# A large fused transformer kernel on one core: 40 blocks of weights under HGRN's levels multiplied in float32 straight from the ring, in place of two float32r parts

## The chip, the cores and the metric

The kernel runs on 1 core of a Trainium2 chip. The metric is the device time of one execution in microseconds (us). Before the change the median of 3 runs is 2754.78 us (2750.23 to 2757.37). Engines are named as in the profile: PE is TensorE (matrix products), PEld its weight load, DVE VectorE, ACT ScalarE, POOL GpSimd, and SP the engine that issues the weight loads from HBM.

## The reference, cut to what matters

Two transformer blocks on 256 tokens of width 1024, all in float32. The change touches the mixer of the second block alone. It projects the normalized input `xn` (256 x 1024) with `w_in` into q, zf_fwd, zf_bwd, v (`inp`), an output gate og, three Hyena channels and two branch gates:

```python
proj = jnp.einsum('bld,dc->blc', xn, w_in)
q, zf_fwd, zf_bwd, inp, og, hy, gates = jnp.split(proj, IN_SPLITS, axis=-1)
```

q goes through Silu, og through Silu and the gates through a sigmoid. zf_fwd and zf_bwd give the decays and keys of HGRN2, a linear attention with a decay per channel (8 heads of 128), run forward and backward over the tokens; its output, per head, is a decayed product of q, keys and v.

## The kernel before, in words

The program is a list of steps in one order, written by a planner in Python. Every engine follows this list and does its own part of each step, in order; semaphores (`Mark`) join the engines. So what an engine does next is fixed by the order of planning, and an instruction that waits holds up all that is planned behind it on its engine.

**Weights.** They come in blocks of 128 x 1024 float32 (512 KB), 8 k-slices of 128 x 128. A block is a `Split` step (L294): SP loads it into one of 3 ring slots (`weight_ring`, L313), ACT rounds it to float32r, the high part (L317), and the remainder, the low part, is a subtraction on DVE (L322) or on POOL (L328), as `c.low_by` says. The two parts go into one of 3 buffers (`weight_parts`). The slot is free again when the low part is made; the buffer, when PE has multiplied the block. `product` (L346 to L351) makes each product as three matmuls: high x high, high x low, low x high. `xn` itself lies as such parts (`acts_high`, `acts_low`), made by `Normalize`; its unrounded value lies in `work`, which nothing reads until HGRN's heads write their output there.

**Jobs.** `submit` (L242) plans the load and split of a block and puts its multiplication in a list; it plans the multiplication of the block that is then more than 2 behind (`AHEAD = 2`). `flush` (L253) plans the first blocks of the next group and all multiplications that are left. `Channels` (L354) multiplies a block into 128 channels x 256 tokens, `TokenUnit` (L393) a block into 2 x 128 tokens x 512 columns (four units make one half of v). `Keep` (L444, its activation at L457) evacuates the bank on ACT. In this stage the blocks have three banks in rotation (`c.rotation = [4, 5, 6]`); banks 0 to 3 belong to HGRN.

**The stage.** In `second_mixer` (L2520) the blocks of zf and zb come first, with the low parts on DVE. Then `c.low_by` is set to "pool", and `together` plans one step of `hgrn` and one step of the filler `more` by turns. `more` submits 40 blocks: 8 of q, 8 of v, then 8 of og and 16 of the two gates (`gate_a`, `gate_b`). `hgrn` (L2165) plans:

- `HgrnKeys`: sigmoids on ACT (L1997, L1998), scalings on DVE (L2007, L2008, L2012), a logarithm on ACT (L2001), once for zf and once for zb;
- `HgrnScan`: 16 scans over the tokens on DVE (L2025, L2026), and a memset on POOL (L2036);
- 9 levels (block sizes 128, 64, 32, 16, 8, 4, 2, 1 and 0), in pairs by `pipeline` with width 2. A level subtracts the decays on DVE (L2067 to L2074), exponentiates them on ACT (L2109, L2111), multiplies them into q and the keys on DVE (L2078, L2081, L2082), makes 16 score products on PE in float32 in two halves of 8 (L2131) and keeps them on DVE (L2097, L2098, L2100); level 0 only adds the keys (L2087);
- 8 `HgrnHead` steps: 4 float32 matmuls each (L2151 to L2154), and a copy to `work` on ACT (L2158).

The filler is out of step with the levels by two blocks (`AHEAD`): behind the scores of the first pair come units 1 to 3 of v and their evacuation, then the exponentials of the second pair; behind those of the third pair come three blocks of og and their evacuations, then the exponentials of the fourth. When the levels are done, 7 blocks are left; before the change they alternate with the heads. Then come the first two splits for Hyena (`w[32]`, `w[40]`), and a barrier (L596).

Of the kernel before, what the change touches and what calls it, by code (L numbers as in the profile page):

```python
# [9 lines left out]
NT, KD = T // P, D // P  # L10
# [89 lines left out]
class Signal:  # L100


    def __init__(self, name, handle, by=1):
        self.name, self.handle, self.by, self.counted, self.sent = name, handle, by, 0, 0
# [19 lines left out]
class Step:  # L124
# [4 lines left out]
    def sync(self, q):  # L129
        pass  # L130
# [30 lines left out]
def pipeline(c, makers, width):  # L161

    makers, active = list(makers), {}
    for slot in range(min(width, len(makers))):
        step = makers.pop(0)(slot)
        active[slot] = [step, step.phases]
    while active:
        for slot in list(active):
            if not active[slot][1]:
                if not makers:  # L170
                    del active[slot]
                    continue
                step = makers.pop(0)(slot)
                active[slot] = [step, step.phases]
            c.plan(active[slot][0])
            active[slot][1] -= 1
        yield


def together(main, filler, every):  # L180

    for n, _ in enumerate(main):
        if n % every == 0:
            next(filler, None)


class Parts:

    def __init__(self, high, low):
        self.high, self.low, self.marks, self.free = high, low, [None] * KD, None


class Core:
# [4 lines left out]
    def __init__(self, nc, ctx, dram):  # L200
        self.nc, self.ctx, self.dram = nc, ctx, dram
        self.steps, self.signals = [], {}
        self.psum = ctx.enter_context(nc.psum_tensor("psum", [P, 4096], F32))
        self.ring = self.sb("weight_ring", [P, self.SLOTS, 1024])
        self.parts = self.sb("weight_parts", [P, self.PARTS, 2, 1024], dtype=F32R)
        self.landed = [self.sig(f"slot_landed_{i}", 16) for i in range(self.SLOTS)]
        self.slot_free = [None] * self.SLOTS
        self.part_free = [None] * self.PARTS
        self.bank_free = [()] * 8
        self.rotation = list(range(7))  # L210
        self.loaded = self.splits = self.n_small = 0
        self.low_by = "vector"
        self.jobs, self.prepared = [], []
        self.small_before = [None] * 16
        self.fence = ()
# [23 lines left out]
    def load(self, out, src, after=()):  # L239
        return self.plan(Load(self, out, src, after)).came  # L240

    def submit(self, src, make):  # L242

        unit = self.prepared.pop(0) if self.prepared else self.plan(Split(self, src)).unit
        self.jobs.append((unit, make))
        if len(self.jobs) > self.AHEAD:
            self.work_off()
# [4 lines left out]

    def flush(self, *following):  # L253
        for src in following:
            self.prepared.append(self.plan(Split(self, src)).unit)
            if self.jobs:
                self.work_off()
        while self.jobs:
            self.work_off()
# [31 lines left out]
    pass  # L291


class Split(Step):  # L294


    def __init__(self, c, src):
        self.src, self.unit = src, Unit()
        u, slot, part = self.unit, c.loaded % c.SLOTS, c.splits % c.PARTS
        c.loaded += 1  # L300
        c.splits += 1
        u.part = part
        self.ring, self.slot_free, self.part_free = c.ring[:, slot, :], c.slot_free[slot], c.part_free[part]
        self.high, self.low = c.parts[:, part, 0, :], c.parts[:, part, 1, :]
        self.low_by = c.low_by
        self.landed = c.landed[slot].next()
        self.rounded = c.mark("weights_high")
        u.ready = c.mark("weights_low_by_" + self.low_by)
        c.slot_free[slot] = u.ready
# [36 lines left out]
def product(q, out, stationary, moving, first, last):  # L346

    (sh, sl), (mh, ml) = stationary, moving
    q.e.matmul(out, sh, mh, start=first, stop=False)  # L349
    q.e.matmul(out, sh, ml, start=False, stop=False)  # L350
    return q.e.matmul(out, sl, mh, start=False, stop=last)  # L351


class Channels(Step):  # L354


    def __init__(self, c, unit, acts, evac):
        self.unit, self.acts, self.evac = unit, acts, evac
        self.weights = c.parts[:, unit.part, :, :].rearrange("p x (k c) -> p x k c", k=KD)
        b = c.take_bank()  # L360
        self.out, self.bank_free = c.bank(b)[:, 0:T], c.bank_free[b]
        self.marks = list(acts.marks)
        self.done = c.part_free[unit.part] = acts.free = c.mark("multiplied")
        c.last_product = self.done
        c.bank_free[b] = (evac.out_of_psum(c),)

    def tensor(self, q):
        w, acts = self.weights, self.acts
        q.wait_ge(self.unit.ready, *self.bank_free)
        for k in range(KD):  # L370
            q.wait_ge(self.marks[k])
            last = product(q, self.out, (w[:, 0, k, :], w[:, 1, k, :]), (acts.high[:, k, :], acts.low[:, k, :]),
                           k == 0, k == KD - 1)
        last.then_inc(*self.done.once())

    def scalar(self, q):
# [16 lines left out]
class TokenUnit(Step):  # L393

    def __init__(self, c, whole, unit, n):
        self.whole, self.unit, self.n = whole, unit, n
        self.weights = c.parts[:, unit.part, :, :].rearrange("p x (k c) -> p x k c", k=whole.n_k)
        if n == 0:
            whole.banks = [c.take_bank() for _ in range(NT)]
            whole.bank_free = [m for b in whole.banks for m in c.bank_free[b]]  # L400
            whole.out = [c.bank(b)[:, 0:whole.cols] for b in whole.banks]
        self.marks = list(whole.acts.marks)
        self.done = c.part_free[unit.part] = whole.acts.free = c.mark("multiplied")
        c.last_product = self.done
        self.final = n == whole.n_units - 1
        if self.final:
            self.evacs = [whole.evac(i) for i in range(NT)]
            for b, evac in zip(whole.banks, self.evacs):
                c.bank_free[b] = (evac.out_of_psum(c),)

    def tensor(self, q):
        whole, w, acts = self.whole, self.weights, self.whole.acts
        q.wait_ge(self.unit.ready)
        if self.n == 0:
            q.wait_ge(*whole.bank_free)
        for i in range(NT):
            tile = slice(P * i, P * i + P)
            for kk in range(whole.n_k):
                k = whole.n_k * self.n + kk
                q.wait_ge(self.marks[k])  # L420
                last = product(q, whole.out[i], (acts.high[:, k, tile], acts.low[:, k, tile]),
                               (w[:, 0, kk, :], w[:, 1, kk, :]), k == 0, k == KD - 1)
        last.then_inc(*self.done.once())

    def scalar(self, q):
# [1711 lines left out]
class HgrnHead(Step):  # L2137


    def __init__(self, c, s, hd, v, o):  # L2140
        self.c, self.s, self.hd, self.v, self.after, self.o = c, s, hd, v, list(s.kept) + list(s.values), o
        self.b = hd % 4
        self.bank_free = c.bank_free[self.b]
        self.mixed, self.taken = c.mark("hg_mixed"), c.mark("hg_taken")
        c.bank_free[self.b] = (self.taken,)
# [8 lines left out]
        q.e.matmul(out[:, P:T], v1, s.at[:, hd, 1, :], start=False, stop=True).then_inc(*self.mixed.once())  # L2154

    def scalar(self, q):
        q.wait_ge(self.mixed)
        q.e.activation(self.o[:, self.hd, :], self.c.bank(self.b)[:, 0:T], ACT.Copy).then_inc(*self.taken.once())  # L2158


# [1 line left out]
    pass  # L2162


def hgrn(c, ctx, s, q, zf, zb, projected, v, o):  # L2165

    lb = c.sb("hg_lb", [P, KD], ctx)
    one_minus = c.sb("hg_one_minus", [P, KD], ctx)
# [22 lines left out]
    s.operands_free, s.kept = [(), ()], [None, None]  # L2191

    yield from pipeline(c, [lambda u, n=n, m=m: HgrnLevel(c, s, n, m, u) for n, m in enumerate([P] + LEVELS + [0])], 2)
    for hd in range(HG_H):
        c.hg_taken = c.plan(HgrnHead(c, s, hd, v, o)).taken
        yield


# [321 lines left out]
def second_mixer(c, h, xn, work, tmp, following):  # L2520

    w = c.dram["w_in_2"]
    with ExitStack() as ctx:
# [6 lines left out]
        with ExitStack() as inner:  # L2530
# [8 lines left out]
                c.channels(w[8 + n], xn, Keep(zf[:, n, :]))  # L2539
            for n in range(KD):  # L2540
                c.channels(w[16 + n], xn, Keep(zb[:, n, :]))
            c.flush(w[0], w[1])
            projected = c.last_kept
            c.rotation = [4, 5, 6]
            c.low_by = "pool"
            s = Hgrn()

            def more():
# [15 lines left out]
                        yield  # L2564

            filler = more()
            together(hgrn(c, inner, s, q, zf, zb, projected, v, o), filler, 1)
            for _ in filler:
                pass
            c.flush(w[32], w[40])  # L2570
            c.barrier()
        gated_ready = c.plan(Activate(c, og[:, :, :], ACT.Silu, c.last_kept)).ready
        for x in (sga, sgb):
# [123 lines left out]
def program(nc, dram, out):  # L2697
    with ExitStack() as ctx:
        c = Core(nc, ctx, dram)
        h = c.sb("h", [P, KD, T])  # L2700
        xn = Parts(*(c.sb(f"acts_{x}", [P, KD, T], dtype=F32R) for x in ("high", "low")))
        work = c.sb("work", [P, KD, T])
        tmp = c.sb("tmp", [P, T])
        c.gains = c.sb("gains", [P, N_GAINS])
        c.ident = c.sb("ident", [P, P])
# [138 lines left out]
```

## Time and profile before

| | |
|---|---|
| median of 3 runs | 2754.78 us |
| the profiled execution | 2750.74 us |
| its span, first to last instruction | 2749.0 us |
| mean granted clock of PE | 0.935 |
| DVE, ACT, POOL busy, share of the span | 65%, 43%, 33% |
| low parts on POOL (L328) | x314, 808.2 us, mean 2582 ns |
| roundings on ACT (L317) | x702, 736.3 us, mean 1049 ns |
| the chain that ended last | PE 75%, DVE 16%, POOL 3%, ACT 3% |

The granted clock is a share of 2.4 GHz; 0.5 is 1.2 GHz. PE's matmuls are pipelined and their records overlap, so the time of one is read from the distance between starts. A float32 matmul leaves two records of weight load and two of multiplication, a float32r matmul one of each.

A row of the timeline has the start in us, the duration in us, the engine, the line, the operation, output <- inputs, the form and how many were merged; in brackets, the idle time before it and what ended it. A row of the chain has start, duration, engine, output and line. A row of the table by stretch of time has the stretch, its length, then busy us (and instructions) of PE, PEld, DVE, ACT and POOL, the granted clock, the share of the DMA engines and GB/s.

### The profile page before, as it was taken

Reading aid. Unit: us, or ns where it says so; the run is one execution under the profiler, and the core shown is the slowest. Engines: PE = TensorE matmul, PEld = TensorE weight load, DVE = VectorE, ACT = ScalarE, POOL = GpSimd, SP = SyncE. Lnnn points to the kernel's source line nnn. Section 1 sums busy time; section 2 is a strip of 40 time slices with the busy share of each in tenths; the row PEclk is TensorE's granted clock in tenths of the full one; section 3 lists DMA queues with packets and bytes.
Section 4 is the critical chain, followed back from the end, with each engine's and each line's share of the span. In section 5 each row is a group of like instructions: output and inputs, shape, how many; then the busy total and the mean of one; then the engine's idle time right before and its main releaser. Section 6 shows DMA issues by size and latency. Waiting matters only on the chain.

```text
span 2749.0 us, 39097 instructions
## 1 busy us (share of the span) xinstructions
PE 2468.2 (90%) x16062; PEld 2233.6 (81%) x16062; DVE 1800.3 (65%) x2703; ACT 1191.1 (43%) x1925; POOL 895.9 (33%) x418
## 2 busy tenths in 40 slices
PE   6866978999999999998867878888999999999997
PEld 5855868999999888886856877578999999888885
DVE  4544444997888655555587547364996888655555
ACT  3422333445444444443544354324445444444443
POOL 2011010797666200001054545110797666200000
PEclk8856988999999999999978898989999999999999
DMA  5210433455444556664422343234455444566663
GB/s 162 92 62 23 125 98 119 150 175 160 146 147 146 165 187 189 188 187 153 123 77 84 101 123 109 85 108 161 146 172 161 147 145 147 168 190 186 189 187 112
DMA packets 108569, 384.41 MB, mean 140 GB/s; under 512 B 13007, under 2 KB 16000, under 8 KB 107816
## 3 DMA queue, kind: packets, MB, share of 16 engines
q1 hardware_dynamic: 108392, 381.91, 45.4%
q8 instruction: 129, 2.11, 0.3%
q14 instruction: 48, 0.39, 0.0%
HBM read 380.79 MB, written 1.06 MB: 139 GB/s over the span
## 4 chain that ended last, share of the span: by engine, by line
PE 75%; DVE 16%; POOL 3%; ACT 3%; issue 2%; DMA 1%; SPq 0%; DVEq 0%; POOLq 0%; ACTq 0%
PE psum L349 21%; PE psum L350 20%; PE psum L351 20%; PE psum L1741 4%; POOL weight_parts L328 2%; PE psum L511 1%; PE psum L2358 1%; PE psum L2131 1%; DVE peer_experts L1649 1%; PE psum L795 1%; PE psum L1220 1%; ACT weight_parts L317 1%; DVE peer_experts L1648 1%; DVE peer_experts L1625 1%; DVE peer_experts L1617 1%
## 5 line engine op out<-in xcount | busy, mean ns | idle before, releaser
L349 PE MATMUL psum<-acts_high,weight_parts 128*128 128x256 f32 x3296 | 972.9, 295 | 65.9 <-DVE acts_low L543 28.4
L328 POOL TENSOR_TENSOR weight_parts<-weight_ring,weight_parts 128x1024 fp32r<-128x1024 f32 x314 | 808.2, 2582 | 551.5 <-ACT weight_parts L317 550.9
L350 PE MATMUL psum<-acts_low,weight_parts 128*128 128x256 f32 x3296 | 945.0, 287 | 0.0
L351 PE MATMUL psum<-acts_high,weight_parts 128*128 128x256 f32 x3296 | 944.0, 286 | 0.0
L317 ACT ACTIVATE weight_parts<-weight_ring 128x1024 fp32r<-128x1024 f32 x702 | 736.3, 1049 | 112.8 <-PE psum L351 109.5
L349 PEld LDWEIGHTS psum<-acts_high,weight_parts 128*128 128x128 f32 x3296 | 643.7, 195 | 83.4 <-issue 42.4
L322 DVE TENSOR_TENSOR weight_parts<-weight_ring,weight_parts 128x1024 fp32r<-128x1024 f32 x388 | 477.0, 1230 | 308.4 <-ACT weight_parts L317 308.4
L350 PEld LDWEIGHTS psum<-acts_low,weight_parts 128*128 128x128 f32 x3296 | 645.5, 196 | 2.4 <-issue 1.7
L351 PEld LDWEIGHTS psum<-acts_high,weight_parts 128*128 128x128 f32 x3296 | 644.4, 196 | 0.0
L349 PE MATMUL psum<-weight_parts,peer_coef 128*128 128x512 f32 x1024 | 405.9, 396 | 4.0 <-issue 3.9
L350 PE MATMUL psum<-weight_parts,peer_coef 128*128 128x512 f32 x1024 | 405.6, 396 | 0.0
L351 PE MATMUL psum<-weight_parts,peer_coef 128*128 128x512 f32 x1024 | 405.6, 396 | 0.0
L1812 ACT ACTIVATE peer_coef<-peer_experts 128x256 fp32r<-128x256 f32 x256 | 106.6, 417 | 363.9 <-PE psum L351 362.8
L489 POOL TENSOR_TENSOR peer_experts<-h 128x256 f32<-128x256 f32 x16 | 9.7, 612 | 746.6 <-DVE h L473 746.4
L1725 DVE TENSOR_TENSOR peer_onehots<-peer_onehots,peer_gates 128x512 f32<-128x512 f32 x128 | 247.9, 1936 | 4.4
L349 PEld LDWEIGHTS psum<-weight_parts,peer_coef 128*128 128x128 f32 x1024 | 192.7, 188 | 51.0 <-issue 4.2
L350 PEld LDWEIGHTS psum<-weight_parts,peer_coef 128*128 128x128 f32 x1024 | 192.9, 188 | 46.8
L351 PEld LDWEIGHTS psum<-weight_parts,peer_coef 128*128 128x128 f32 x1024 | 192.8, 188 | 46.6
L1816 DVE TENSOR_TENSOR peer_coef<-peer_experts,peer_coef 128x256 fp32r<-128x256 f32 x256 | 109.6, 429 | 161.2 <-ACT peer_coef L1812 161.2
L1722 DVE TENSOR_TENSOR peer_onehots<-psum,peer_pairs 128x1024 f32<-128x1024 f32 x128 | 155.2, 1212 | 0.1
L1789 ACT ACTIVATE psum<-psum 128x4 f32<-128x4 f32 (+25 forms) x156 | 41.4, 266 | 248.7 <-PE psum L351 248.7
L1791 ACT ACTIVATE peer_experts<-psum 128x256 f32<-128x256 f32 (+32 forms) x250 | 79.3, 317 | 151.2 <-PE psum L351 151.1
(382 smaller groups left out, 2426.3 us busy)
## 6 DMA issues: line engine op xcount, KB each, us to landing
weight_ring<-in_peer_down SPq DMA_DIRECT2D x128, 512.0 KB, 3.6
weight_ring<-in_peer_up SPq DMA_DIRECT2D x128, 512.0 KB, 3.6
weight_ring<-in_peer_u SPq DMA_DIRECT2D x128, 512.0 KB, 3.6
weight_ring<-in_peer_v SPq DMA_DIRECT2D x128, 512.0 KB, 4.1
weight_ring<-in_w_in SPq DMA_DIRECT2D x88, 512.0 KB, 3.6
weight_ring<-in_w_out SPq DMA_DIRECT2D x16, 512.0 KB, 3.5
weight_ring<-in_peer_w_q SPq DMA_DIRECT2D x16, 512.0 KB, 3.6
weight_ring<-in_w_in_v SPq DMA_DIRECT2D x10, 512.0 KB, 3.5
```

The source lines that it names most:

```text
L317: q.e.activation(self.high, self.ring, ACT.Copy).then_inc(*self.rounded.once())
L322: q.e.tensor_tensor(self.low, self.ring, self.high.bitcast(F32), ALU.subtract).then_inc(*self.unit.ready.once())
L328: q.e.tensor_tensor(self.low, self.ring, self.high.bitcast(F32), ALU.subtract).then_inc(*self.unit.ready.once())
L349: q.e.matmul(out, sh, mh, start=first, stop=False)
L350: q.e.matmul(out, sh, ml, start=False, stop=False)
L351: return q.e.matmul(out, sl, mh, start=False, stop=last)
L1722: q.e.tensor_tensor(self.hot, over(over(self.c.bank(7)[:, 0:P], GROUP, 1), 2, 1), over(x.pairs[:, :, tokens], P, 3), ALU.is_equal).then_in ...
L1725: q.e.tensor_tensor(self.hot[:, 0, :, :], self.hot[:, 0, :, :], over(x.gates[:, tokens], P, 2), ALU.mult).then_inc(*self.ready.once())
L1741: last = q.e.matmul(out, self.hot[:, 0, t, :], self.hot[:, 1, t, :], start=True, stop=True)
L1791: last = q.e.activation(self.x.experts[:, self.n, n:T], out[:, n:T], ACT.Gelu_apprx_tanh)
L1812: q.e.activation(self.high, self.src, ACT.Copy).then_inc(*self.rounded.once())
L1816: q.e.tensor_tensor(self.low, self.src, self.high.bitcast(F32), ALU.subtract).then_inc(*self.ready.once())
```

## The change

The 40 blocks of the filler are planned as `Whole` steps: SP loads them into the ring, and nothing else is done to them. PE multiplies them in float32 from the ring slot with the unrounded activations in `work` (`xn.whole`); one matmul stands where three stood. The slot is free again only when PE has multiplied the block. `c.whole` is set before the first two blocks of q are prepared, and taken back in `finish`, which `hgrn` now calls between the levels and the heads: it plans what is left of the filler (7 blocks) and the two splits for Hyena, whose low parts are made by POOL. So all heads come behind the last block. Since a head writes to `work`, its copy on ACT waits for the last whole block (`o_free`).

```diff
@@ class Core @@
+    def fetch(self, src):
+        return self.plan(Whole(self, src) if self.whole else Split(self, src)).unit
+
     def submit(self, src, make):
-        unit = self.prepared.pop(0) if self.prepared else self.plan(Split(self, src)).unit
+        unit = self.prepared.pop(0) if self.prepared else self.fetch(src)
...
+class Whole(Step):
+    def __init__(self, c, src):
+        self.src, self.unit = src, Unit()
+        slot = c.loaded % c.SLOTS
+        c.loaded += 1
+        self.ring, self.slot_free = c.ring[:, slot, :], c.slot_free[slot]
+        self.unit.whole, self.unit.slot, self.unit.ready = self.ring, slot, c.landed[slot].next()
+
+    def sync(self, q):
+        q.wait_ge(self.slot_free)
+        q.e.dma_start(self.ring, self.src).then_inc(*self.unit.ready.once())
...
@@ class Channels @@
-        self.done = c.part_free[unit.part] = acts.free = c.mark("multiplied")
+        self.done = c.mark("multiplied")
+        if unit.whole is None:
+            self.weights = c.parts[:, unit.part, :, :].rearrange("p x (k c) -> p x k c", k=KD)
+            c.part_free[unit.part] = acts.free = self.done
+        else:
+            self.weights = unit.whole.rearrange("p (k c) -> p k c", k=KD)
+            c.slot_free[unit.slot] = acts.whole_free = self.done
...
-            last = product(q, self.out, (w[:, 0, k, :], w[:, 1, k, :]), (acts.high[:, k, :], acts.low[:, k, :]),
-                           k == 0, k == KD - 1)
+            if self.unit.whole is None:
+                last = product(q, self.out, (w[:, 0, k, :], w[:, 1, k, :]), (acts.high[:, k, :], acts.low[:, k, :]),
+                               k == 0, k == KD - 1)
+            else:
+                last = q.e.matmul(self.out, w[:, k, :], acts.whole[:, k, :], start=k == 0, stop=k == KD - 1)
...
@@ class TokenUnit @@
+                    last = q.e.matmul(whole.out[i], acts.whole[:, k, tile], w[:, kk, :], start=k == 0,
+                                      stop=k == KD - 1)
...
@@ class HgrnHead @@
     def scalar(self, q):
-        q.wait_ge(self.mixed)
+        q.wait_ge(self.mixed, self.o_free)
...
@@ def hgrn @@
     yield from pipeline(c, [lambda u, n=n, m=m: HgrnLevel(c, s, n, m, u) for n, m in enumerate([P] + LEVELS + [0])], 2)
+    o_free = finish()
     for hd in range(HG_H):
-        c.hg_taken = c.plan(HgrnHead(c, s, hd, v, o)).taken
+        c.hg_taken = c.plan(HgrnHead(c, s, hd, v, o, o_free)).taken
         yield
...
@@ def second_mixer @@
+            c.whole = True
             c.flush(w[0], w[1])
             projected = c.last_kept
             c.rotation = [4, 5, 6]
-            c.low_by = "pool"
...
-            together(hgrn(c, inner, s, q, zf, zb, projected, v, o), filler, 1)
-            for _ in filler:
-                pass
-            c.flush(w[32], w[40])
+
+            def finish():
+                for _ in filler:
+                    pass
+                c.whole = False
+                c.low_by = "pool"
+                c.flush(w[32], w[40])
+                return xn.whole_free
+
+            together(hgrn(c, inner, s, q, zf, zb, projected, v, o, finish), filler, 1)
             c.barrier()
```

## Rows read from the trace of the kernel before

**Rows 1.** The page's first part: busy time of each engine over the span.
```profile
PE 2468.2 (90%) x16062; PEld 2233.6 (81%) x16062; DVE 1800.3 (65%) x2703; ACT 1191.1 (43%) x1925; POOL 895.9 (33%) x418
```

**Rows 2.** Busy time by stretch of time: the columns, the stage, one block at 1381.
```profile
core 0: us, PE busy (x) PEld busy (x) DVE busy (x) ACT busy (x) POOL busy (x), PEclk, DMA share, GB/s
1363.00:1598.00 235.00, 169.19 (x1192) 162.46 (x1191) 157.39 (x131) 103.08 (x112) 116.41 (x40) 0.83 0.29 88
...
1381.00:1386.00 5.00, 4.96 (x24) 4.70 (x23) 2.99 (x6) 2.93 (x3) 0.00 (x0) 0.52 0.32 105
```

**Rows 3.** Timeline of DVE and of POOL among the scans.
```profile
1399.89 1.80 POOL L2036 MEMSET hg_scores<- 128x2048 f32 x1
1401.66 5.48 POOL L328 TENSOR_TENSOR weight_parts<-weight_ring,weight_parts 128x1024 fp32r<-128x1024 f32 x2
...
1401.01 0.66 DVE L2026 TENSOR_TENSOR_SCAN hg_bb<-reset,hg_zb 128x256 f32<-128x256 f32 x1
1402.17 2.83 DVE L2026 TENSOR_TENSOR_SCAN hg_bb<-reset,hg_zb 128x256 f32<-128x256 f32 x1
```

**Rows 4.** Timeline of DVE and of POOL in the second pair of levels.
```profile
1451.39 2.28 DVE L2078 TENSOR_TENSOR hg_zf<-hg_q,hg_zf 128x2048 f32<-128x2048 f32 x1
...
1458.03 4.44 DVE L2078 TENSOR_TENSOR hg_q<-hg_q 128x2048 f32<-128x2048 f32 x1
...
1454.44 10.23 POOL L328 TENSOR_TENSOR weight_parts<-weight_ring,weight_parts 128x1024 fp32r<-128x1024 f32 x3 [7.46 <-ACT weight_parts L317]
```

**Rows 5.** Waits in the stage: who waited for whom, total, times, longest.
```profile
PE psum L349 <- POOL weight_parts L328: 15.3, 2, 12.8
```

**Rows 6.** The chain of waits: one float32r product; 16 float32 matmuls of 512 columns.
```profile
1549.11 0.12 PE psum L349
...
1762.03 13.75 PE psum L2358 x32
```

**Rows 7.** Timeline of PE: first and last of 27 rows of Hyena, float32, 256 columns.
```profile
1799.45 0.59 PE L2432 MATMUL psum<-sin_js,filters 128*128 128x256 f32 x2
...
1810.67 0.59 PE L2432 MATMUL psum<-sin_js,filters 128*128 128x256 f32 x2
```

**Rows 8.** The page's last part, DMA issues: w_in's blocks, KB each, us to landing.
```profile
weight_ring<-in_w_in SPq DMA_DIRECT2D x88, 512.0 KB, 3.6
```

**Rows 9.** Timeline of ACT: the two logarithms, and the fourth pair's first exponential.
```profile
1375.09 1.91 ACT L2001 ACTIVATE hg_zf<-hg_zf 128x2048 f32<-128x2048 f32 x1 [1.28 <-DVE hg_zf L2012]
...
1383.07 1.91 ACT L2001 ACTIVATE hg_zb<-hg_zb 128x2048 f32<-128x2048 f32 x1 [4.85 <-DVE hg_zb L2012]
...
1517.34 1.91 ACT L2109 ACTIVATE hg_zf<-hg_zf 128x2048 f32<-128x2048 f32 x1
```

**Rows 10.** Timeline of DVE: after the scans, and where each next pair begins.
```profile
1409.47 0.69 DVE L2067 COPY hg_zf<-hg_bf 128x1024 f32<-128x1024 f32 x1
...
1437.93 1.20 DVE L2070 TENSOR_TENSOR hg_zf<-hg_bf 128x1024 f32<-128x1024 f32 x1
...
1481.31 1.21 DVE L2070 TENSOR_TENSOR hg_zf<-hg_bf 128x1024 f32<-128x1024 f32 x1
...
1498.19 1.22 DVE L2082 TENSOR_TENSOR hg_k<-hg_kb,hg_k 128x1024 f32<-128x1024 f32 x1
...
1509.64 1.20 DVE L2070 TENSOR_TENSOR hg_zf<-hg_bf 128x1024 f32<-128x1024 f32 x1
...
1550.37 2.27 DVE L2087 TENSOR_TENSOR hg_zb<-hg_kf,hg_kb 128x2048 f32<-128x2048 f32 x1
```

**Rows 11.** The chain of waits: scoring halves, and POOL's queue ahead of the barrier.
```profile
1426.67 3.68 PE psum L2131 x16
...
1557.75 1.78 PE psum L2131 x16
...
1598.64 2.48 POOLq L596
```

**Rows 12.** Groups by line between 1799 and 1810 us: Hyena's weight loads.
```profile
L2432 PEld LDWEIGHTS psum<-sin_js,filters 128*128 128x128 f32 x26 | 4.9, 190 | 0.7
```

More of the change, by code:

```diff
@@ L187, with __init__ @@
 class Parts:
-    def __init__(self, high, low):
+    def __init__(self, high, low, whole=None):
         self.high, self.low, self.marks, self.free = high, low, [None] * KD, None
+        self.whole, self.whole_free = whole, None
 class Core:
@@ L212, in __init__ @@
         self.low_by = "vector"
+        self.whole = False
         self.jobs, self.prepared = [], []
@@ L254, in flush @@
         for src in following:
-            self.prepared.append(self.plan(Split(self, src)).unit)
+            self.prepared.append(self.fetch(src))
             if self.jobs:
@@ L301, in __init__ @@
         c.splits += 1
-        u.part = part
+        u.part, u.whole = part, None
         self.ring, self.slot_free, self.part_free = c.ring[:, slot, :], c.slot_free[slot], c.part_free[part]
@@ L358, in __init__ @@
         self.unit, self.acts, self.evac = unit, acts, evac
-        self.weights = c.parts[:, unit.part, :, :].rearrange("p x (k c) -> p x k c", k=KD)
         b = c.take_bank()
@@ L396, in __init__ @@
         self.whole, self.unit, self.n = whole, unit, n
-        self.weights = c.parts[:, unit.part, :, :].rearrange("p x (k c) -> p x k c", k=whole.n_k)
         if n == 0:
@@ L402, in __init__ @@
         self.marks = list(whole.acts.marks)
-        self.done = c.part_free[unit.part] = whole.acts.free = c.mark("multiplied")
+        self.done = c.mark("multiplied")
+        if unit.whole is None:
+            self.weights = c.parts[:, unit.part, :, :].rearrange("p x (k c) -> p x k c", k=whole.n_k)
+            c.part_free[unit.part] = whole.acts.free = self.done
+        else:
+            self.weights = unit.whole.rearrange("p (k c) -> p k c", k=whole.n_k)
+            c.slot_free[unit.slot] = whole.acts.whole_free = self.done
         c.last_product = self.done
@@ L420, in tensor @@
                 q.wait_ge(self.marks[k])
-                last = product(q, whole.out[i], (acts.high[:, k, tile], acts.low[:, k, tile]),
-                               (w[:, 0, kk, :], w[:, 1, kk, :]), k == 0, k == KD - 1)
+                if self.unit.whole is None:
+                    last = product(q, whole.out[i], (acts.high[:, k, tile], acts.low[:, k, tile]),
+                                   (w[:, 0, kk, :], w[:, 1, kk, :]), k == 0, k == KD - 1)
+                else:
+                    last = q.e.matmul(whole.out[i], acts.whole[:, k, tile], w[:, kk, :], start=k == 0,
+                                      stop=k == KD - 1)
         last.then_inc(*self.done.once())
@@ L2137, with __init__ @@
 class HgrnHead(Step):
-    def __init__(self, c, s, hd, v, o):
+    def __init__(self, c, s, hd, v, o, o_free):
         self.c, self.s, self.hd, self.v, self.after, self.o = c, s, hd, v, list(s.kept) + list(s.values), o
+        self.o_free = o_free
         self.b = hd % 4
@@ L2162, with hgrn @@
     pass
-def hgrn(c, ctx, s, q, zf, zb, projected, v, o):
+def hgrn(c, ctx, s, q, zf, zb, projected, v, o, finish):
     lb = c.sb("hg_lb", [P, KD], ctx)
@@ L2702, in program @@
         work = c.sb("work", [P, KD, T])
+        xn.whole = work
         tmp = c.sb("tmp", [P, T])
```

## The prediction, on record before the change was run

> **What bounds the kernel now.** I read the busy table first: over the span of 2749.0 us TensorE (PE) is busy 90% [rows 1]. That is an average, so I read the stage that the diff touches by itself, from the last block of zb at 1362 us to the barrier behind the heads at 1601 us, 239 us. There PE is busy only 169 of 235 us at a granted clock of 0.83, VectorE (DVE) 157, GpSimd (POOL) 116 and ScalarE (ACT) 103 [rows 2]. No engine fills the stage; work is handed from one to the next, so I followed the chain of waits there and then the timeline of DVE.
>
> The chain is: DVE scales, ACT takes the logarithm, DVE scans, and then four pairs of levels follow one another; in each DVE subtracts, ACT exponentiates, DVE multiplies, PE scores, DVE keeps. The timeline of DVE shows what makes the chain long. A scan takes 0.66 us, but 2.83 where it meets a low-part subtraction of POOL [rows 3]; in the second pair one 128x2048 product takes 2.28 us and the next 4.44, under three subtractions that fill 10.23 us of POOL [rows 4]. I count 18 such operations on DVE in the stage: 1 scaling, 7 scans, 5 in the second pair of levels and 5 in the fourth. Each loses about 2.2 us (2.83 less 0.66; 4.44 less 2.28), 39 us in all. The memset on POOL is no such case: a scan under it keeps its 0.66 us [rows 3]. PE loses too: 15.3 us at L349 waiting for POOL's low parts, 12.8 of it at once [rows 5].
>
> **What the change removes and adds.** Removed: 40 roundings on ACT (1.05 us), 40 subtractions on POOL (2.4 us where undisturbed), and with them the 18 collisions. Added: nothing but time on PE. Before, a block is 24 products of 256 columns at 0.12 us [rows 6], 2.88 us. After, it is 8 float32 matmuls. Hyena's are of that form (float32, 128x128 by 256 columns): each leaves two records, and from 1799.45 to 1810.67 there are 26 of them in 11.22 us [rows 7], 0.432 each, so a block costs 3.45. A unit of v has 4 matmuls of 512 columns; 16 of that form took 13.75 us (32 records) [rows 6], 0.86 each, 3.44 a unit. On PE that is +0.57 us for each of 32 blocks and about +0.7 for the 8 units: 24 us more work, to be set against 39 us of collisions plus waits. What counts is what lies on the chain, so I walk it.
>
> **From 1362 to the scans.** q0 to q2 run at once (three free banks, three loads long landed; a load takes 3.6 us [rows 8]) and end at 1372.3. q3 needs q0's bank, which ACT frees behind the first logarithm (1375.09 and 1.91 [rows 9]), at 1377; having idled, PE is at the lower clock, as at 1381 where the granted clock was 0.52 and 24 products filled 4.96 us [rows 2]; q3 ends near 1383. The slowed scaling ends 2.1 us sooner, so the second logarithm (before at 1383.07 [rows 9]) ends at 1382.9, not 1384.98. 16 scans at a pitch of 0.58 (0.66 each, overlapping a little) end at 1392.3, where before they ended at 1409.4 [rows 10]: 17 us sooner. q4 to q7 run back to back, ending at 1397.0; now they are late, not the scans. ACT evacuates q7, loads a table, applies Silu, loads another (5 us together); the first exponential starts at 1402.0, the fourth ends at 1409.3, and DVE ends its products at 1412.9 (before 1426.5, where PE's second halves start [rows 11]). PE has idled again, so the first two scoring halves run at 1.2 GHz and cost 3.7 us each against 1.78 at 2.4 GHz [rows 11]; one unit of v (3.44) and the second halves (3.6) follow.
>
> **The pairs**, by when DVE begins the next pair (before in [rows 10]):
> - Pair 1: 1424.9, before 1437.93. Gain 13.
> - Pair 2: its exponentials stand behind v's evacuation on ACT, and so behind three units of v: 3 x 3.44 us, then 1.0. DVE's last product ends at 1446.0, undisturbed. Then PE binds: half a pair 1.8, two units 6.9, two halves 3.6. 1459.5, before 1481.31. Gain 22.
> - Pair 3: undisturbed before, 12 operations of DVE in 18 us (1481.31 to 1499.4), and so after. 1487.7, before 1509.64. Gain 22.
> - Pair 4: DVE 18 us instead of 29; but its exponentials wait behind the evacuation of a third block (as at 1517.34 [rows 9]), 3 x 3.45 us, so 2.3 us of this are given back. 1518.3, before 1550.37. Gain 32.
> - The tail is PE alone: 14 blocks x 0.57 gives back 8 us. The heads move behind the last block at no cost (PE runs in order either way: 8 x 0.9 us). The two splits for Hyena move ahead of the heads, onto idle engines; today the barrier waits for the second (POOL's queue, to 1601.1 [rows 11]). PE ends at 1576.1, the last head is copied by 1576.5, and the barrier follows 24.5 us sooner.
>
> Costed at nothing: the heads' new wait for the last whole block (that block ends before the first head on PE itself). Ring slots are now held until the multiplication, but three slots give a load 6.9 us against 3.6 to land. The memset moves ahead of the stage, under DVE's normalization: nothing by [rows 3], at most one collision of 2.2 us.
>
> **Sum.** The profiled execution took 2750.74 us (span 2749.0 and 1.74 around it), 4.0 under the median of 2754.78. It would become 2726.2; the median 2754.8 - 24.5 = 2730.
>
> One rule speaks against the change. In the trace, the 190 ns weight load of a Hyena float32 record [rows 12] lies under the multiplication, since records start every 0.216 us [rows 7]. The Trainium skill ("TensorE: Matmul & The Clock Gate", The mechanism) says that a weight load overlaps a running matmul only where it takes other rows of the array; these take all rows. By that rule the sum would turn into rival C. The trace does not agree.
>
> **Rivals.**
> A. The clock costs more. PE gets short idles (at 1443.8, 1468.7, 1474.9 and 1505.6 by the walk, 2 to 4.5 us). If three of them drop the clock, each costs up to 2.5 us on what follows (a block then 5.4 instead of 2.88, by 1381 [rows 2]): gain 17, 2738. For it: the stage's clock of 0.83. Against: most of these idles are short, and part of the slow work would end inside the next idle. 0.17.
> B. The clock costs less: PE is denser, q3 and pair 1's first halves (4 us) and an evacuation or two slip. Gain 30, 2725. 0.12.
> C. Slower: the weight loads of float32 blocks from the ring are exposed. 16 records x 0.19 = 3.0 us a block, on the 29 blocks and units that my walk puts on the chain: +88 - 24.5, so 2818. It decides from 4.3 us a block (24.5 / 29 = 0.84 over 3.45). For it, only that no block so far is multiplied from the ring in float32; against it, all 26 matmuls of Hyena. 0.04.
> D. DVE is slowed not by POOL but by something that stays (loads, PE). Then the 39 us stay and PE's cost comes on top: about 5 us slower, 2760. Against it: the clean round of pair 3 has PE and loads beside it, and POOL's one subtraction in it was the one that waited. 0.03.
> The forecast has 0.64.
>
> **Range.** 0.3% is 8 us, about what a measurement of this kernel can tell from no change. The forecast's own spread is 5 us either way (the ACT waits and the clock are each worth 2 to 4); A and B reach to 2741 and 2719. That holds 0.85 to 0.9. Faster by over 0.3%: the forecast, B and nearly all of A, 0.91. Within: 0.04. Slower: 0.05.
>
> **What would show it.** Right: no L317 or L328 in the stage but two each at its end; DVE's scans all near 0.66 and its products at 1.2 and 2.28; blocks 3.45 us apart; the stage near 215 us with PE above 175 busy; DVE's next pairs at the times above, less whatever shifts the stage's start. A pair that begins later names its step: exponentials late behind evacuations, or scoring halves at 3.7 us. Wrong: a pitch of blocks over 4 us (C), or slow operations on an idle POOL (D).

## The result, and the profile after

The changed kernel takes 2736.07 us (median of 6 runs, 2731.28 to 2742.75) against 2752.31 for the kernel before: ratio 0.9943, 95% interval 0.9926 to 0.996, 16 us faster. (Each ratio in this document is the one on record, worked out from all runs of both kernels in that comparison; it is not exactly the quotient of the two medians beside it.) The profile's page, against [rows 1]:

```profile
PE 2489.4 (91%) x15774; PEld 2227.7 (81%) x15774; DVE 1759.3 (64%) x2701; ACT 1152.3 (42%) x1885; POOL 784.0 (29%) x380
...
L348 POOL TENSOR_TENSOR weight_parts<-weight_ring,weight_parts 128x1024 fp32r<-128x1024 f32 x276 | 696.2, 2531 | 642.0 <-ACT weight_parts L337 641.5
```

PE is 21 us busier in a span 14 us shorter. POOL made 314 low parts before and makes 276 here. That is 38 fewer, where the prediction has 40: the low parts of the first two blocks of q were made by DVE before (x388 there, x386 now).

The stage itself, against [rows 2]. The table by stretch of time, and a short stretch of the third pair:

```profile
core 0: us, PE busy (x) PEld busy (x) DVE busy (x) ACT busy (x) POOL busy (x), PEclk, DMA share, GB/s
1365.00:1582.00 217.00, 187.71 (x930) 155.51 (x928) 118.59 (x131) 68.04 (x77) 4.71 (x2) 0.93 0.33 102
1475.00:1480.00 5.00, 3.75 (x16) 3.50 (x17) 5.00 (x5) 0.00 (x0) 0.00 (x0) 0.50 0.00 0
```

From 239 us it fell to 216, with PE busy 188 us at a granted clock of 0.93 (0.83 before), and POOL busy for 4.7 us (116 before), the two splits for Hyena. DVE's busy time fell by 39 us, the sum that the prediction gave the 18 collisions. Set side by side in their order, the 131 DVE instructions of the stage differ in exactly 18 places, each by 2.0 to 2.2 us, 38.7 us in all. DVE's timeline, against [rows 3] and [rows 10]:

```profile
1387.97 0.67 DVE L2063 TENSOR_TENSOR_SCAN hg_bb<-reset,hg_zb 128x256 f32<-128x256 f32 x1
...
1395.66 0.69 DVE L2104 COPY hg_zf<-hg_bf 128x1024 f32<-128x1024 f32 x1
...
1426.97 1.21 DVE L2107 TENSOR_TENSOR hg_zf<-hg_bf 128x1024 f32<-128x1024 f32 x1
...
1461.83 1.21 DVE L2107 TENSOR_TENSOR hg_zf<-hg_bf 128x1024 f32<-128x1024 f32 x1
...
1492.50 1.20 DVE L2107 TENSOR_TENSOR hg_zf<-hg_bf 128x1024 f32<-128x1024 f32 x1
...
1523.29 2.28 DVE L2124 TENSOR_TENSOR hg_zb<-hg_kf,hg_kb 128x2048 f32<-128x2048 f32 x1
```

Every scan takes 0.67 us. The stage began 3.2 us later than before in this profile, so I count from its first step on ACT (`hg_t`) to the activation behind the barrier (`hg_og`). Timeline of ACT, the kernel before:

```profile
1363.67 0.22 ACT L1982 ACTIVATE hg_t<-hg_t 128x16 f32<-128x16 f32 x1
...
1602.58 1.91 ACT L2207 ACTIVATE hg_og<-hg_og 128x2048 f32<-128x2048 f32 x1
```

and the changed kernel:

```profile
1366.88 0.22 ACT L2019 ACTIVATE hg_t<-hg_t 128x16 f32<-128x16 f32 x1
...
1583.09 1.91 ACT L2247 ACTIVATE hg_og<-hg_og 128x2048 f32<-128x2048 f32 x1
```

| us from the stage's start | before | forecast | after | error |
|---|---|---|---|---|
| scans done | 45.8 | 28.6 | 28.8 | +0.2 |
| pair 2 begins | 74.3 | 61.2 | 60.1 | -1.1 |
| pair 3 begins | 117.6 | 95.8 | 95.0 | -0.8 |
| pair 4 begins | 146.0 | 124.0 | 125.6 | +1.6 |
| level 0 | 186.7 | 154.6 | 156.4 | +1.8 |
| behind the barrier | 238.9 | 214.4 | 216.2 | +1.8 |

The stage gained 22.7 us where 24.5 were forecast. The chain of waits after shows what it consists of now (start, duration, engine and what):

```profile
1380.63 20.02 PE psum L401 x80
...
1475.56 3.75 PE psum L2168 x16
1480.03 3.75 PE psum L2168 x16
...
1491.26 10.38 PE psum L401 x48
1502.04 1.81 ACT hg_zf L2146
...
1539.45 34.53 PE psum L401 x160
1581.80 1.28 ACT L2247
```

L401 is a block in float32. 80 records are 40 matmuls, the five blocks q3 to q7, in 20.02 us: 2.8 over five times 3.45, the price of q3's start at the lower clock. The prediction has the same price: from 1377 to 1397.0 is 20.0 us. 160 are ten blocks in 34.53 us, 3.45 each. The exponentials of the fourth pair (1502.04) stand behind three blocks (1491.26), as forecast. The two rows at 1475.56 and 1480.03 are the place where the walk missed by most (2.5 us).

### The profile page after: what moved, and what is told of

It reads as the page before. It is cut to its first block, busy times and chain, and to the rows that moved or that the text cites. A ratio compares the mean times of both kernels' runs of the same rounds, so it can differ in the third digit from the quotient of the medians.

```text
span 2734.7 us, 38435 instructions
## 1 busy us (share of the span) xinstructions
PE 2489.4 (91%) x15774; PEld 2227.7 (81%) x15774; DVE 1759.3 (64%) x2701; ACT 1152.3 (42%) x1885; POOL 784.0 (29%) x380
## 4 chain that ended last, share of the span: by engine, by line
PE 78%; DVE 13%; ACT 3%; POOL 3%; issue 2%; DMA 1%; SPq 0%; DVEq 0%; POOLq 0%; ACTq 0%
PE psum L369 20%; PE psum L370 20%; PE psum L371 20%; PE psum L1778 4%; PE psum L401 3%; POOL weight_parts L348 2%; PE psum L548 1%; PE psum L2168 1%; PE psum L2398 1%; PE psum L458 1%; PE psum L832 1%; DVE peer_experts L1686 1%; PE psum L1257 1%; DVE peer_experts L1685 1%; DVE peer_experts L1662 1%
## 5 line engine op out<-in xcount | busy, mean ns | idle before, releaser
L369 PE MATMUL psum<-acts_high,weight_parts 128*128 128x256 f32 x3040 | 898.3, 296 | 50.0 <-DVE acts_low L580 28.4
L348 POOL TENSOR_TENSOR weight_parts<-weight_ring,weight_parts 128x1024 fp32r<-128x1024 f32 x276 | 696.2, 2531 | 642.0 <-ACT weight_parts L337 641.5
L370 PE MATMUL psum<-acts_low,weight_parts 128*128 128x256 f32 x3040 | 871.4, 287 | 0.0
L371 PE MATMUL psum<-acts_high,weight_parts 128*128 128x256 f32 x3040 | 870.6, 286 | 0.0
L337 ACT ACTIVATE weight_parts<-weight_ring 128x1024 fp32r<-128x1024 f32 x662 | 695.3, 1051 | 79.7 <-PE psum L371 70.9
L369 PEld LDWEIGHTS psum<-acts_high,weight_parts 128*128 128x128 f32 x3040 | 593.9, 195 | 67.0 <-issue 43.1
L370 PEld LDWEIGHTS psum<-acts_low,weight_parts 128*128 128x128 f32 x3040 | 595.6, 196 | 2.5 <-issue 1.7
L371 PEld LDWEIGHTS psum<-acts_high,weight_parts 128*128 128x128 f32 x3040 | 594.5, 196 | 0.0
```

What stands on the lines that cost most here:

```text
L337: q.e.activation(self.high, self.ring, ACT.Copy).then_inc(*self.rounded.once())
L348: q.e.tensor_tensor(self.low, self.ring, self.high.bitcast(F32), ALU.subtract).then_inc(*self.unit.ready.once())
```

## The experiments

**Both kernels once more.** For a second profile of each, and a narrower interval.

> The kernel before, unchanged, for a second profile. The stage between the last block of zb and the barrier behind the heads should again take 239 us, with DVE's scans slowed under POOL's subtractions. If the 3.2 us by which the stage began later in the changed kernel, and the 4.6 us lost behind it, are scatter of the clock, the times outside the stage differ by some us between this profile and the first one of the same kernel. If they belong to the change, the two profiles agree outside the stage.

> The changed kernel, unchanged, for a second profile and a narrower interval. Theory (collisions of POOL with DVE gone, at the price of PE's four passes): stage again 217 us (216 to 219), 22 us under before; total 0.993 to 0.995 of before. If the 7 us lost outside the stage are scatter, the total should drift towards the stage's gain, 0.992; if they are systematic, it stays near 0.994 and the second profile loses them at the same places.

The ends of the stage in the second profiles, timeline of ACT, the kernel before:

```profile
1367.19 0.22 ACT L1982 ACTIVATE hg_t<-hg_t 128x16 f32<-128x16 f32 x1
...
1606.10 1.91 ACT L2207 ACTIVATE hg_og<-hg_og 128x2048 f32<-128x2048 f32 x1
```

and the changed kernel:

```profile
1370.39 0.22 ACT L2019 ACTIVATE hg_t<-hg_t 128x16 f32<-128x16 f32 x1
...
1586.60 1.91 ACT L2247 ACTIVATE hg_og<-hg_og 128x2048 f32<-128x2048 f32 x1
```

The differences are 238.91 and 216.21 us, to the hundredth those of the first two profiles (238.91 and 216.21). The stage repeats; what surrounds it does not. The two profiled executions of the kernel before differ by 10 us (2750.74 and 2760.71), 3.5 of it ahead of the stage, 6.4 behind it, and none inside. So the 3.2 us ahead of the stage and the 5 us behind it, by which the first comparison fell short of 22.7, are within the scatter of one kernel. That no part of them belongs to the change is not shown: from `hg_og` to the end the kernel before took 1146.4 and 1152.8 us, the changed kernel 1151.6 both times. The second comparison gave 2736.01 against 2755.79, ratio 0.9921 (0.9905 to 0.9937): 19.8 us between the medians, 21.8 by the ratio (17 to 26), and the stage's 22.7 lies within that.

**POOL's subtraction taken from the kernel before.**

```diff
-        u.ready = c.mark("weights_low_by_" + self.low_by)
+        u.ready = self.rounded if self.low_by == "none" else c.mark("weights_low_by_" + self.low_by)
...
+            c.low_by = "none"
             c.flush(w[0], w[1])
```

> The kernel before without POOL's subtraction for the 40 blocks (the low parts of the weights are stale ones, so the third product of each uses wrong data); PE still makes three float32r products a block and ACT still rounds. Theory: all 18 collisions go and PE's price is not paid, so it gains more than the change does: pairs of levels of about 28.5 us each, a tail of 51, stage 202 to 207, total 2752 - 35 = 2717 (2710 to 2724). Rival D (DVE is slowed by something else, such as loads or PE): scans of 2.8 us and products of 3.4 and 4.4 stay, total within 5 us of before.

2722.03 us, ratio 0.9878 (0.9859 to 0.9897): 33.8 us faster. Timeline of DVE:

```profile
1382.66 0.67 DVE L2026 TENSOR_TENSOR_SCAN hg_bb<-reset,hg_zb 128x256 f32<-128x256 f32 x1
1383.24 0.67 DVE L2025 TENSOR_TENSOR_SCAN hg_bf<-reset,hg_zf 128x256 f32<-128x256 f32 x1
...
1433.28 2.29 DVE L2078 TENSOR_TENSOR hg_zf<-hg_q,hg_zf 128x2048 f32<-128x2048 f32 x1 [0.77 <-ACT hg_zf L2109]
...
1437.76 2.28 DVE L2078 TENSOR_TENSOR hg_q<-hg_q 128x2048 f32<-128x2048 f32 x1
```

No scan and no product is slow, though ACT rounds, the loads run and PE multiplies as before. The stage took 203.8 us. So POOL's part (its collisions with DVE and PE's waits for it) is worth 35.1 us, and what the change pays for it in PE's time, net of ACT's roundings, is the other 12.4 of 216.2. Of these 7.6 lie in the tail (59.8 us from level 0 on, against 52.2). The pairs themselves were not of 28.5 us each, as I had expected, but of 31.9, 33.0, 27.9 and 30.1. (The edit also drops DVE's two low parts ahead of the stage.) Rival D falls.

**POOL's subtraction added to the changed kernel.**

```diff
+    def pool(self, q):
+        if self.junk is not None:
+            q.wait_ge(self.unit.ready, self.part_free, self.before)
+            q.e.tensor_tensor(self.out, self.x, self.high.bitcast(F32), ALU.subtract).then_inc(*self.junk.once())
```

> The changed kernel with one subtraction of 128x1024 on POOL for 38 of the 40 blocks, started when the block has landed; it reads the activations and a buffer, writes a buffer that nobody reads, and nobody waits for it. Theory: the collisions come back on DVE alone (10 to 20 of them at 2.2 us), less the slack that DVE now has ahead of the exponentials: 20 to 35 us slower than the changed kernel, 2756 to 2771. Rival D or a gain that came from ACT's freed time: no change from 2736.

2773.97 us, ratio 1.0056 (1.0037 to 1.0076): 38 us slower than the changed kernel, and slower than the kernel before. Timeline of DVE and POOL in the fourth pair:

```profile
1526.94 2.93 POOL L325 TENSOR_TENSOR weight_parts<-work,weight_parts 128x1024 fp32r<-128x1024 f32 x1 [4.90 <-DMA weight_ring<-in_w_in]
1527.58 3.38 DVE L2131 TENSOR_TENSOR hg_q<-hg_bb 128x1024 f32<-128x1024 f32 x1
1530.27 2.91 POOL L325 TENSOR_TENSOR weight_parts<-work,weight_parts 128x1024 fp32r<-128x1024 f32 x1 [0.40 <-DMA weight_ring<-in_w_in]
1530.88 3.38 DVE L2133 TENSOR_TENSOR hg_k<-hg_bf 128x1024 f32<-128x1024 f32 x1
1533.74 2.75 POOL L325 TENSOR_TENSOR weight_parts<-work,weight_parts 128x1024 fp32r<-128x1024 f32 x1 [0.56 <-DMA weight_ring<-in_w_in]
1534.19 3.39 DVE L2134 TENSOR_TENSOR hg_k<-hg_bb 128x1024 f32<-128x1024 f32 x1
1537.30 2.49 POOL L325 TENSOR_TENSOR weight_parts<-work,weight_parts 128x1024 fp32r<-128x1024 f32 x1 [0.81 <-DMA weight_ring<-in_w_in]
1537.50 4.44 DVE L2138 TENSOR_TENSOR hg_zf<-hg_q,hg_zf 128x2048 f32<-128x2048 f32 x1
```

ACT is planned to wait for the last of these subtractions, behind the 40 blocks, but no wait for POOL shows there, and nothing else waits for them. Such a subtraction lengthens the DVE operation that starts under it, mostly by 2.0 to 2.2 us. I had expected 10 to 20 DVE operations to be slowed; 25 were, by 49.0 us in all: 21 by 2.0 to 2.2 us, and 4 by 1.0 to 1.2. Four lie in pair 3, which was clean before. The four small ones tell what DVE loses. They began 1.0 to 1.3 us behind the start of a subtraction of 2.4 us, and lost about what was left of it:

```profile
1481.87 2.36 POOL L325 TENSOR_TENSOR weight_parts<-work,weight_parts 128x1024 fp32r<-128x1024 f32 x1 [1.13 <-DMA weight_ring<-in_w_in]
1483.07 2.24 DVE L2130 TENSOR_TENSOR hg_zf<-hg_bf 128x1024 f32<-128x1024 f32 x1
```

The operation takes 1.2 us when it is undisturbed. The stage took 256.7 us, 40.5 over the changed one; not all of the 49.0 lies on the chain. The collisions by themselves are worth more than the whole gain: float32 blocks on PE with POOL still at work are 18 us slower than the kernel before.

**The order alone**, heads behind the last block and the splits ahead of them, in the kernel before.

```diff
     yield from pipeline(c, [...], 2)
+    finish()
     for hd in range(HG_H):
...
```

> The kernel before with only the change of order: the rest of the filler and Hyena's two splits planned between the levels and the heads, the 40 blocks still as float32r parts. Theory: PE runs the same work in order, and the barrier no longer waits for POOL's second split: 1 us faster to no change, 2751 (2748 to 2754 within the scatter of the runs). Rival: the order itself carries part of the gain (over 3 us), or costs it.

2755.19 against 2755.93 us, ratio 1.0004 (0.9989 to 1.0019); the stage took 238.4 us, 0.5 less. The order carries none of the gain.

**The tail split again.** In the changed kernel the last 12 of the 40 blocks go back to float32r parts.

```diff
+                        if (first, n) == (56, 4):
+                            c.whole, c.low_by = False, "pool"
```

> The changed kernel with the last 12 of the 40 blocks as float32r parts again, low parts on POOL. They are multiplied behind DVE's last subtractions, where PE alone sets the time. Theory: each costs 2.88 us instead of 3.45 and meets next to nothing on DVE: 6.8 us faster than the changed kernel, stage 210 us, 2729. Rival: the split's extra wait for ACT and POOL, or collisions with the last keeps and level 0's sum, eat it: within 2 us of the changed kernel.

2727.05 us, ratio 0.9883 (0.9865 to 0.9902). The stage took 209.3 us (1366.37 to 1575.64 on the same two steps of ACT), 6.9 less than with the change: 12 x 0.57. From here on the intervals of the totals overlap from one version to the next, so what tells the versions apart is the length of the stage, read from one profile of each. One operation of DVE collides (level 0's sum, 4.36 us) and has the slack for it.

**Exponentials ahead of the evacuations**, in all pairs, on top of the last.

```diff
         if self.m:
-            yield
             q.wait_ge(self.q_parted)
...
+        yield
```

> As the last one, and the exponentials of each pair planned on ACT with DVE's subtractions, ahead of the evacuations of the blocks that now hold them up (2.9 us of DVE's idle time in the second pair, 2.2 in the fourth; the first pair's now go ahead of Silu). Theory: 4 to 5 us faster than the kernel with split tail, 2724 to 2725. Rival: the wait moves to PE, whose banks are evacuated later behind the exponentials, or Silu comes later and holds the first products: no gain, or a loss of up to 4 us.

2729.54 us, ratio 0.99 (0.9884 to 0.9917); stage 209.6 us. No gain: the rival. Pair 4 became 2.2 us shorter, 28.6 instead of 30.8, and so did pair 3, but now Silu stands behind four exponentials, and DVE's first products wait for it:

```profile
1396.34 2.29 DVE L2115 TENSOR_TENSOR hg_zf<-hg_q,hg_zf 128x2048 f32<-128x2048 f32 x1 [5.81 <-ACT hg_q L2247]
```

Pair 1 lost 3.9 us by that, pair 2 another 0.9.

**The same for the last two pairs only.**

```diff
         if self.m:
-            yield
+            if self.m > 8:
+                yield
...
+        yield
```

> As the kernel with the split tail, but only the exponentials of levels 8, 4, 2 and 1 are planned with the subtractions; the first two pairs keep the order of the changed kernel. Theory, from the last run's pairs (28.5 us for the third and fourth, against 30.7 and 30.8): stage 209.3 - 2.2 - 2.2 = 204.9 us, total 2722 to 2723. Rival: the gain of the third pair there came from its other starting point (PE's clock), not from the order; then 207 us, 2725.

2727.23 us, ratio 0.9914 (0.9885 to 0.9943); stage 207.0 us. The rival again: pair 4 kept its 2.2 us, and pair 3 stayed at 30.7. Its exponentials had not been late. Its shorter run in the last experiment went with PE's clock: the second level's first half took 2.02 us there and 3.75 here, as in the changed kernel. PE had idled 4.6 us ahead of the pair's scores in all three. The chain of the last experiment, against the two rows of 3.75 us above:

```profile
1467.14 3.46 PE psum L2168 x16
1471.61 2.02 PE psum L2168 x16
```

So the same idle time does not always cost the same; why the clock came back sooner there is open.

**One block into pair 3's idle time.**

```diff
-    together(hgrn(...), filler, 1, {})
+    together(hgrn(...), filler, 1, {22: 1})
```

(The dictionary says how many steps more the filler takes at which step.)

> As the last one, and the filler takes one step more ahead of the third pair's scores, where PE idles 4.6 us in the changed kernel and then runs both scoring halves at 1.2 GHz (3.75 us each, not 1.8). Theory: the clock stays up and the tail is a block shorter: stage 202 to 203 us, total 2720. Rival: the halves wait for the fourth block, whose bank ACT frees only behind the exponentials, and the clock was not what made this pair long: no gain.

2719.9 us, ratio 0.9878 (0.9847 to 0.9909); stage 202.2 us, as forecast. The chain in pair 3:

```profile
1472.04 5.38 PE psum L402 x16
1477.42 3.57 PE psum L2171 x32
```

The fourth block, at 1472.04, still meets the lower clock and takes 5.38 us; then both first halves together run in 3.57 us, where they took 3.75 each. Pair 3 took 28.7 us instead of 30.7 although it holds a block more, and the tail is 2.9 us shorter.

**Two units of v into pair 1's idle time**, in place of that block.

```diff
-    together(hgrn(...), filler, 1, {22: 1})
+    together(hgrn(...), filler, 1, {10: 2})
```

(In these last two the tail is split from one and two blocks later on, so that the first split stays behind DVE's products.)

> As the one before the last, and the filler takes two steps more ahead of the first pair's scores, where PE idles 11.6 us: two units of v run there, and v's evacuation, which held up the second pair's exponentials (DVE idle for 2.9 us), comes sooner. Theory: tail two blocks shorter (5.8 us), second pair 3 us shorter, third pair up to 3.5 us longer, since five blocks lie in it instead of three: stage 199 to 201 us, total 2717 to 2718. Rival: banks and ACT's order give it back; no better than 204.

2710.12 us against 2751.18, ratio 0.985 (0.9822 to 0.9878): the best version, 41 us under the kernel before. The stage took 190.9 us, 8 to 10 less than I expected. The chain in the first two pairs:

```profile
1420.14 3.43 PE psum L2171 x16
1423.57 3.44 PE psum L459 x8
1427.01 3.57 PE psum L2171 x32
1430.58 3.45 PE psum L459 x8
1434.05 0.61 ACT hg_v L495
...
1434.79 13.97 PE psum L459 x32
1448.76 7.14 PE psum L2171 x64
```

One unit stands ahead of v's evacuation instead of three, and the two units that lay between the halves of pair 2 (1450.16 to 1457.02 in the changed kernel, 6.9 us) are gone from there: pair 2 took 25.3 us instead of 34.9. I had counted the first and forgotten the second. Pair 3 also went the other way: with five blocks in it PE did not idle ahead of its scores, and it took 28.5 us instead of 30.7, where I had allowed for up to 3.5 more. The tail is 5.8 us shorter, as expected, and pair 1 is 1.4 longer.

## Why the prediction was right, and where it was not

- **What bounds the stage.** That DVE was held up by POOL, 18 times at 2.2 us, is shown from both sides: without POOL's subtraction 35.1 us of the stage go (PE's waits for POOL among them), with it 40.5 come back. That POOL made 38 of the 40 low parts, and not all, changes nothing in this.
- **PE's price.** 3.45 us a block by Hyena's rows [rows 7], 3.45 measured. The rule that would expose each weight load (rival C) does not hold here: the ten blocks of the tail have 0.432 us a matmul, Hyena's pace, with 190 ns of weight load in each of its two records. The Trainium skill's sentence on the overlap of weight loads ("TensorE: Matmul & The Clock Gate", The mechanism) is, taken alone, contradicted by the 34.53 us above: 160 records with a load of 190 ns each take 30.4 us for the loads alone, which would leave 26 ns for each multiplication. The same section lets a load into a background weight buffer overlap as well; no run here shows which buffer these loads go to. The measurement decides.
- **The walk.** Every hand-over came where it was forecast, within 1.8 us: q3 behind the first logarithm, pair 2's exponentials behind v's evacuation, pair 4's behind a third block, the tail on PE.
- **The step that failed** is the clock in pair 3 (rival A, in one place). PE had idled 4.6 us ahead of its scores (1470.98 to 1475.56), the granted clock was 0.50, and both halves took 3.75 us where the walk had 1.8. That is the +2.5 us between pair 3 and pair 4 in the table, and a block in the idle time took 1.9 of them away. Idle time alone does not set this price: in the kernel before PE idled 6.4 us ahead of the same scores, and the second half took 2.02 us. In pair 1 it went the other way by 1.1: the second half ran partly at the upper clock (2.02 us, forecast 3.7).
- **The total.** 2736 instead of 2730, 16.2 us under the median before instead of 24.5: 1.8 us from the stage. The rest lies outside it and is of the size of the scatter, since the second comparison gives 19.8 to 21.8 us with the same stage; a small loss of the change outside the stage is not excluded.
- **Costed at nothing.** The new order, heads behind the last block and splits ahead of them, cost nothing (0.5 us gained). The memset now lies at 1311 us, and the heads' new wait never ends last.

## What to carry to other kernels

A cheaper form on the bound engine can be the dearer one, if what prepares its operands blocks another engine: here one fifth more time on PE for a block (3.45 us for 2.88) took 39 us off DVE and, net, 22.7 off the stage. Use the exact form only where the preparation collides, and the split form where it has a free engine; in this stage that was worth 6.9 us more. When an in-order engine idles before its part of a chain, move work planned for the tail in there: it was the largest step behind the change itself (16 us), more than the 11.6 us of idle time, because units also left the chain behind it. All these gains are of one stage of 239 us: the best version takes 48 us off it, and the kernel is 1.5% faster by it.

## What was not expected

The stage repeated to 0.01 us in two profiles of each kernel, 238.91 and 216.21, while the whole executions differed by 10 and 3.5 us. Where a change stays in one stage, the distance between its two ends is by far a sharper measure than the total. And a subtraction on POOL can lose as well as win. In the chain of the kernel before, one that came behind the start of pair 3's products took 8.21 us, and DVE was not slowed at all (one of 8.19 us in pair 1 did the same); where POOL came first it took 2.4 to 2.8 among the scans, and DVE was the one that waited. The longer one:

```profile
1493.43 8.21 POOL weight_parts L328
```
